# First step of each expert loop fed by products with zero-one tiles instead of gathered rows

## The chip, the core and the metric

The kernel runs on one core of one Trainium2 chip. The metric is the device time of one launch in microseconds (us), less is better; of several runs the median counts.

## What is computed

Two token groups (512 prompt tokens and 32 sample tokens, width 1024) go through two layers. Each layer is a mixer followed by a mixture of experts: a router picks, for every token, the best of four expert groups and in it two of its four experts; each of the 16 experts is a gated two-layer network of inner width 512. All of it is float32. Cut to the part that the change touches:

```python
def _moe(h, w_router, b_router, w_gate, w_up, w_down):
    ...                                   # softmax, best group, top 2 in it, weights -> combine
    for e in range(N_EXPERTS):
        act = jax.nn.silu(h @ w_gate[e]) * (h @ w_up[e])
        term = combine[..., e:e + 1] * (act @ w_down[e])
        y = term if y is None else y + term
    return y
```

The kernel does not multiply every token with every expert: it sorts the 2 x 544 picks by expert and multiplies only those rows.

## The kernel before, in words

The work of one layer's experts is 13 **steps** (PATTERN, L54). A "B" step takes up to 128 rows of one expert, a "P" step takes up to 64 rows of each of two experts. The order of the experts over the steps is found at run time from their counts, but expert 0 is always the first place and expert 1 the second (L581-582).

**Routing.** `pick(layer)` and `places(layer)` (L1589, L1640) run on VectorE (DVE) as one long chain of small operations. In its first part `places` finds each pick's row in the sorted order (`picked(0, selv)`, L1662: `posf` in float, `posi` in integers, and it raises `rows_ready`). Its second part finds the order of the experts over the steps, the rows of the outputs and a table `tabi` for the other engines; its last instruction (L1713) raises `pos_ready`.

**Gathering the rows.** On GpSimd (POOL) `dispatch(layer)` (L624) waits for `rows_ready`, then issues ten indirect DMAs that scatter the token rows of `h` into the sorted buffer `xs_d` in DRAM. When all have landed and `pos_ready` is up, `load_x(0)` and `load_x(1)` fetch the rows of steps 0 and 1 into the two halves of `xg`, which lie on the first two tiles of `h`. In layer 0 `load_ab(2)` follows: five broadcast loads (three of 512 KB, two of 128 KB) of the next norm's scale, shift and gain, needed only after the expert loop (`scale_ready(2)`, L1751). Then for each step n: `load_x(n + 2)` once TensorE has turned the rows of step n, then the store of step n's outputs to `ys_d` when ScalarE and VectorE have copied them. All of these are in one DMA queue (q0), in this order.

**Products.** On TensorE (PE) `experts(layer)` (L873) does for each step n: `pe_up(n)`; `tokens(n + 1)`, which waits for the rows and turns them with eight 128x128 transposes (`pe_tx`, L818, the rows taken at a stride of 8 columns); the first half of `pe_gate(n + 1)`; `pe_th(n)`; the second half of `pe_gate(n + 1)`; `pe_down(n)`. Ahead of the loop stand `tokens(0)` and `pe_gate(0)`. ScalarE and VectorE each copy one half of the turned rows from PSUM to `xgT` (`copy_x`); on VectorE this copy stands behind all of `places`.

In layer 0 TensorE still has products of the conditioning vectors to do (`ada`, L746) between routing and experts: `ada(6)` may start when VectorE has done `stage_ada(4)`, which stands in VectorE's program behind `places(0)`; `experts(0)` starts when VectorE has done `stage_ada(6)`.

**Weights.** SyncE (SP) feeds six slots of 2 MB in queue q1, two each for gate, up and down. For layer 0 it loads g0 and u0 when the last `ada` weights free their slots, then waits for the rows of step 1 (`xg_loaded[1]`, L451), then issues g1, d0, u1 and d1; every further load waits until the step that used its slot is through (`refill`, L457). In layer 1 all six first loads are issued before the routing. The weights are read as "(p k) f": partition p takes eight neighbouring rows, 16 KB in one piece, which is why the rows are turned at a stride of 8.

Of the kernel before, what the change touches and what calls it, by code (L numbers as in the profile page):

```python
# [12 lines left out]
def bass_yoco_stream_step(  # L13
# [7 lines left out]
    ALU, ACT, AX = mybir.AluOpType, mybir.ActivationFunctionType, mybir.AxisListType  # L21

    P = 128
# [12 lines left out]
    KC = D // P  # L36
# [73 lines left out]
    with ctx:  # L110
# [3 lines left out]
        def sem(name):  # L114
            return ctx.enter_context(nc.semaphore(name))
# [20 lines left out]
        hact = hf[:, 4608:5120]  # L136
        hactT = hT_raw[:, 0:512].rearrange("p (k t) -> p k t", k=KE)
        ysb = hT_raw[:, 512:2560].rearrange("p (b n) -> p b n", b=2)
        pair_w = hT_raw[:, 2560:3072].rearrange("p (a i j) -> p a i j", a=2, i=NE)

        rf = ring[:, :, :].rearrange("p s n -> p (s n)")
# [12 lines left out]
        S_sb = rf[:, 14336:16384].rearrange("p (b n) -> p b n", b=4)  # L154
        partT_f = rf[:, 13312:13312 + TOK]
        mf = mod[:, :, :, :].rearrange("p a s d -> p (a s d)")
        ck = [v.rearrange("p (t n) -> p t n", t=CT) for v in (mf[:, 0:2048], rf[:, 16384:18432])]
        cv = [v.rearrange("p (t n) -> p t n", t=CT) for v in (mf[:, 2048:4096], rf[:, 8192:10240])]
        bias_s = [mf[:, 4096:4096 + (CT + 1) * P], rf[:, 10240:10240 + (CT + 1) * P]]
# [125 lines left out]
        rank_done = sem("rank_done")  # L285
        rows_ready = sem("rows_ready")
        pos_ready = sem("pos_ready")
        scattered = sem("scattered")
        xg_loaded = [sem(f"xg{i}_loaded") for i in range(2)]
        y_stored = [sem(f"y{i}_stored") for i in range(2)]  # L290
# [113 lines left out]
        def _(sp):  # L404
# [21 lines left out]
            def experts(layer):  # L426
# [8 lines left out]
                def first(kind, e):  # L435

                    view, slot = views[kind][0], views[kind][1] + e
                    if layer == 0:
                        last = max(n for n in range(NADA) if ada_slot[n] == slot)
                        sp.wait_ge(unit_used, last + 1)  # L440
                    elif kind == "g":
                        sp.wait_ge(o_done, 2 * NT)
                    else:
                        sp.wait_ge(tr_done, 2 * (turned(5, TS) + 1))
                        sp.wait_ge(ab_loaded, 80 * 5)
                    load(slot, w(view, e))
# [75 lines left out]
        def _(pool):  # L522
# [99 lines left out]
            load_g(1)  # L622

            def dispatch(layer):  # L624
                pool.wait_ge(rows_ready, layer + 1)
                pool.wait_ge(tail_stored, 16)
                for t in range(NT):
# [14 lines left out]
                pool.wait_ge(scattered, 16 * 2 * NT * (layer + 1))  # L642
                pool.wait_ge(pos_ready, layer + 1)
                b = layer * NSTEP
                load_x(0)
                load_x(1)
                if layer == 0:
                    load_ab(2)

                for n in range(NSTEP):  # L650
                    if layer == 0 and n == NSTEP - 2:
                        for j in range(0, NOV, TP):
                            m = min(TP, NOV - j) * P
# [89 lines left out]
        def _(pe):  # L743
# [74 lines left out]
            def pe_tx(g, par):  # L818

                for half, done in enumerate((E.xt_act, E.xt_dve)):  # L820
# [3 lines left out]
                        last = T.transpose(pb[half][:, c * P:(c + 1) * P], xg[:, par, 4 * half + c:D:KC], ident[:, :])  # L824
                    last.then_inc(E.tx, 1)

            def tile_product(bank, lhs, rhs, start, stop):

                if len(rhs) == 1:
                    return T.matmul(bank[:, :], lhs, rhs[0], start=start, stop=stop)  # L830
                for a in range(2):
                    last = T.matmul(bank[HALF * a:HALF * a + HALF, :], lhs[:, HALF * a:HALF * a + HALF], rhs[a],  # L832
                                    start=start, stop=stop, tile_position=(0, HALF * a))
                return last

            def pe_gate(g, par, ws, ks):
                for k in ks:
                    if k == 0:
                        pe.wait_ge(E.xt_act, g + 1)
                        pe.wait_ge(E.xt_dve, g + 1)  # L840
                        if g:
                            pe.wait_ge(E.silu, g)
                    last = tile_product(pb[3], xgT[:, par, k, :], [w[:, k * DE:(k + 1) * DE] for w in ws],
                                        k == 0, k == KC - 1)
                if ks[-1] == KC - 1:
                    last.then_inc(E.gate, 1)

            def pe_up(g, par, ws):
                if g:
                    pe.wait_ge(E.hact, g)  # L850
                for k in range(KC):
                    last = tile_product(pb[4], xgT[:, par, k, :], [w[:, k * DE:(k + 1) * DE] for w in ws],
                                        k == 0, k == KC - 1)
                last.then_inc(E.up, 1)

            def pe_th(g):
                pe.wait_ge(E.hact, g + 1)
                for c in range(KE):
                    last = T.transpose(pb[2][:, c * P:(c + 1) * P], hact[:, c:DE:KE], ident[:, :])  # L859
                last.then_inc(E.th, 1)  # L860

            def pe_down(g, ws):
# [10 lines left out]
            def experts(layer):  # L873
# [7 lines left out]

                def tokens(n):
                    g = b + n
                    loads = sum(len(STEP_PLACES[i % NSTEP]) for i in range(g % 2, g + 1, 2))
# [284 lines left out]
        def _(act):  # L1169
# [84 lines left out]
            def experts(layer):  # L1254
                b = layer * NSTEP

                def copy_x(g):
                    act.wait_ge(E.tx, 2 * g + 1)
                    if g >= 2:
                        act.wait_ge(E.up, g - 1)  # L1260
                    A.activation(xgT[:, g % 2, 0:4, :], pb[0][:, :].rearrange("p (c t) -> p c t", c=4),  # L1261
                                 ACT.Copy).then_inc(E.xt_act, 1)

                copy_x(b)
                for g in range(b, b + NSTEP):
                    act.wait_ge(E.gate, g + 1)
                    if g:
                        act.wait_ge(E.hact, g)
                    A.activation(sg, pb[3][:, :], ACT.Silu).then_inc(E.silu, 1)
# [205 lines left out]
        def _(dve):  # L1475
# [164 lines left out]
            def places(layer):  # L1640
# [74 lines left out]
            def experts(layer):  # L1715
                b = layer * NSTEP

                def copy_x(g):
                    dve.wait_ge(E.tx, 2 * g + 2)
                    if g >= 2:  # L1720
                        dve.wait_ge(E.up, g - 1)
                    V.tensor_copy(xgT[:, g % 2, 4:8, :], pb[1][:, :].rearrange("p (c t) -> p c t", c=4)).then_inc(E.xt_dve, 1)  # L1722

                copy_x(b)
                for g in range(b, b + NSTEP):
                    dve.wait_ge(E.silu, g + 1)
                    dve.wait_ge(E.up, g + 1)
                    if g:
                        dve.wait_ge(E.th, g)
                    V.tensor_tensor(hact, pb[4][:, :], sg, ALU.mult).then_inc(E.hact, 1)  # L1730
                    if g + 1 < b + NSTEP:
                        copy_x(g + 1)
                    if g >= 2:
# [322 lines left out]
```

## Time and profile before

| | |
|---|---|
| median of 3 runs | 1416.54 us (1414.11 to 1419.67) |
| the profiled execution's own time | 1414.6 us |
| its span, first to last instruction | 1413.1 us, mean granted TensorE clock 0.902 |
| busy: TensorE / VectorE / ScalarE / GpSimd | 80% / 29% / 16% / 14% of the span |
| DMA traffic | 365.5 MB, mean 259 GB/s |

The span is one execution on the core; all moments below are microseconds from its start. The two expert loops are the stretches from 211 to 537 (layer 0) and from 1064 to 1378 (layer 1). A busy share over the whole span says little here: the stages have different limits, so the rows are read by stage.

### The profile page before, as it was taken

The page shows a single profiled execution, that of the slowest core. Times are in us where ns is not written, and L with a number is a line of the kernel's source. Part 1 is how long each engine was busy: PE and PEld are TensorE (multiplying, and loading weights), DVE is VectorE, ACT ScalarE, POOL GpSimd, SP SyncE. Part 2 cuts the span into 40 slices and gives each one's busy share as a digit, 9 for nine tenths or more (in the row PEclk, how much of TensorE's full clock was granted, in tenths as well). Part 3 has the DMA queues.
Part 4 walks back from the last instruction along what each step waited for, and adds up shares of the span by engine and source line. Part 5 has one row for each costly group of instructions (what it writes and reads, how often), then busy time and mean ns, then how long its engine had stood idle before and what let it go on. Part 6 is the DMA issues. An engine that isn't in the chain of part 4 may idle for free.

```text
span 1413.1 us, 12206 instructions
## 1 busy us (share of the span) xinstructions
PE 1128.2 (80%) x4592; PEld 544.1 (39%) x4592; DVE 409.1 (29%) x870; ACT 232.7 (16%) x489; POOL 191.3 (14%) x328
## 2 busy tenths in 40 slices
PE   1639856899999992999998698679727999999990
PEld 0117413344444341444554344454413444444340
DVE  1153660000101004536316555323560000000005
ACT  1002200010101002212112465211201000000001
POOL 6000021000000002000010763210020000000002
PEclk8669778999999996899999799979957999999995
DMA  9999599999899995112242401817235899998835
GB/s 314 395 385 393 224 407 362 396 424 382 348 428 344 386 341 204 52 60 65 90 178 83 121 1 40 262 39 286 104 143 182 311 424 359 372 427 336 352 125 205
DMA packets 55240, 365.52 MB, mean 259 GB/s; under 512 B 7215, under 2 KB 7711, under 8 KB 36156
## 3 DMA queue, kind: packets, MB, share of 16 engines
q1 hardware_dynamic: 32512, 285.79, 51.4%
q0 software_dynamic: 21104, 78.40, 16.1%
q8 instruction: 38, 0.62, 0.2%
q10 hardware_dynamic: 1564, 0.53, 0.1%
q14 instruction: 22, 0.18, 0.0%
HBM read 335.09 MB, written 34.33 MB: 261 GB/s over the span
## 4 chain that ended last, share of the span: by engine, by line
PE 69%; DVE 11%; DMA 10%; POOL 4%; issue 3%; ACT 2%; SPq 0%; ACTq 0%; POOLq 0%; DVEq 0%
PE pb L830 29%; PE pb L995 15%; PE pb L832 9%; DMA ring<-in_ada_w_dram 2%; DMA gainb<-in_norm_g_dram 2%; PE pb L824 2%; POOL ring L725 2%; PE pb L771 2%; DMA ring<-in_w_gate_dram 1%; DMA ada_d<-stage 1%; POOL xs_d L629 1%; DVE h L1722 1%; PE pb L1142 1%; DVE h L1531 1%; PE pb L1087 1%
## 5 line engine op out<-in xcount | busy, mean ns | idle before, releaser
L830 PE MATMUL pb<-ring,h 128*128 128x512 f32 x640 | 290.1, 603 | 19.6 <-DVE h L1722 19.6
L995 PE MATMUL pb<-ring,hT_raw 128*128 128x512 f32 x512 | 225.5, 598 | 2.7 <-DVE x L1558 1.5
L830 PEld LDWEIGHTS pb<-ring,h 128*128 128x128 f32 x640 | 119.9, 193 | 162.6 <-issue 162.6
L830 PE MATMUL pb<-ring,hT_raw 128*128 128x512 f32 x320 | 141.4, 594 | 1.5 <-issue 1.5
L995 PEld LDWEIGHTS pb<-ring,hT_raw 128*128 128x128 f32 x512 | 96.7, 192 | 118.6 <-issue 114.6
L1736 DVE COPY hT_raw<-pb 128x512 f32<-128x512 f32 x26 | 18.0, 692 | 382.1 <-PE pb L830 292.3
L757 PE MATMUL pb<-ring,cT 128*32 128x512 f32 x448 | 73.1, 795 | 69.2 <-DMA ring<-in_ada_w_dram 56.2
L832 PE MATMUL pb<-ring,h 128*64 128x512 f32 x384 | 88.1, 606 | 9.4 <-DVE h L1722 4.9
L661 POOL DMA_DIRECT2D ys_d<-hT_raw x26 | 14.1, 541 | 576.7 <-DVE hT_raw L1736 576.7
L830 PEld LDWEIGHTS pb<-ring,hT_raw 128*128 128x128 f32 x320 | 60.1, 190 | 79.4 <-issue 79.4
L1730 DVE TENSOR_TENSOR h<-pb,h 128x512 f32<-128x512 f32 x26 | 18.0, 692 | 182.8 <-PE pb L830 144.8
L1261 ACT ACTIVATE h<-pb 128x512 f32<-128x512 f32 x26 | 15.5, 597 | 312.4 <-PE pb L824 312.4
L757 PEld LDWEIGHTS pb<-ring,cT 128*32 128x32 f32 x448 | 15.8, 132 | 119.8 <-DMA ring<-in_ada_w_dram 58.4
L771 PE MATMUL pb<-ident,h 128*128 128x128 f32 (+1 forms) x160 | 28.4, 329 | 41.5 <-DVE h L1534 31.4
L824 PE MATMUL pb<-ident,h 128*128 128x128 f32 x208 | 29.7, 289 | 34.1 <-DMA h<-xs_d 34.1
L725 POOL TENSOR_TENSOR ring<-gainb,ring 128x128 f32<-128x128 f32 (+3 forms) x64 | 53.4, 861 | 19.8 <-DVE mx L1914 19.7
L832 PEld LDWEIGHTS pb<-ring,h 128*64 128x64 f32 x384 | 27.7, 138 | 60.3 <-issue 59.6
L824 PEld LDWEIGHTS pb<-ident,h 128*128 128x128 f32 x208 | 27.7, 193 | 48.7 <-DMA h<-xs_d 24.7
L771 PEld LDWEIGHTS pb<-ident,h 128*128 128x128 f32 (+1 forms) x160 | 23.7, 200 | 51.4 <-DVE h L1534 37.0
L832 PE MATMUL pb<-ring,hT_raw 128*64 128x512 f32 x192 | 42.5, 595 | 0.0
L1277 ACT ACTIVATE hT_raw<-pb 128x512 f32<-128x512 f32 x26 | 15.5, 597 | 162.6 <-PE pb L830 123.7
L1273 ACT ACTIVATE hT_raw<-pb 128x512 f32<-128x512 f32 x26 | 15.5, 597 | 147.2 <-PE pb L859 147.2
(323 smaller groups left out, 1152.5 us busy)
## 6 DMA issues: line engine op xcount, KB each, us to landing
ring<-in_w_gate_dram SPq DMA_DIRECT2D x32, 2048.0 KB, 10.6
ring<-in_w_up_dram SPq DMA_DIRECT2D x32, 2048.0 KB, 11.5
ring<-in_w_down_dram SPq DMA_DIRECT2D x32, 2048.0 KB, 12.3
ring<-in_ada_w_dram SPq DMA_DIRECT2D x24, 2048.0 KB, 10.7
ys_d<-hT_raw POOLq DMA_DIRECT2D x26, 512.0 KB, 10.5
h<-xs_d POOLq DMA_DIRECT2D x20, 512.0 KB, 15.5
ring<-in_kv_ada_w_dram SPq DMA_DIRECT2D x4, 2048.0 KB, 10.9
ring<-in_w_kvf_dram SPq DMA_DIRECT2D x4, 2048.0 KB, 16.6
```

Source lines behind the costliest of these rows:

```text
L725: g.tensor_tensor(nfm[s][b], maskp[:, SEQ - w:SEQ], nfb[:, 2 * j + s, 0:b + 1, :].rearrange("p t k -> p (t k)"), ALU.subtract).then_inc(at ...
L757: last = T.matmul(bank[32 * j:32 * j + 32, :], cT[:, 2 * u + k, :], w[:, k, j, :], start=(u == 0 and k == 0), stop=(u == 3 and k == 1), ti ...
L771: last = T.transpose(pb[2 + b][:, c * P:c * P + rows[t]], half_cols(src, t, 4 * b + c), ident[0:rows[t], 0:rows[t]])
L824: last = T.transpose(pb[half][:, c * P:(c + 1) * P], xg[:, par, 4 * half + c:D:KC], ident[:, :])
L830: return T.matmul(bank[:, :], lhs, rhs[0], start=start, stop=stop)
L832: last = T.matmul(bank[HALF * a:HALF * a + HALF, :], lhs[:, HALF * a:HALF * a + HALF], rhs[a], start=start, stop=stop, tile_position=(0, H ...
L995: last = T.matmul(bank[:, :], hT[:, k, col[t]:col[t] + P], w[:, k * 512:(k + 1) * 512], start=(k == 0), stop=(k == KC - 1))
L1261: A.activation(xgT[:, g % 2, 0:4, :], pb[0][:, :].rearrange("p (c t) -> p c t", c=4), ACT.Copy).then_inc(E.xt_act, 1)
L1273: A.activation(hactT, pb[2][:, :].rearrange("p (c t) -> p c t", c=KE), ACT.Copy).then_inc(E.hactT, 1)
L1277: A.activation(ysb[:, g % 2, 0:512], pb[5][:, :], ACT.Copy).then_inc(E.ys_act, 1)
L1730: V.tensor_tensor(hact, pb[4][:, :], sg, ALU.mult).then_inc(E.hact, 1)
L1736: V.tensor_copy(ysb[:, g % 2, 512:1024], pb[6][:, :]).then_inc(E.ys_dve, 1)
```

## The change

For step 0 of each layer the rows are no longer gathered through DRAM. VectorE builds five zero-one tiles `oneh` right behind `rows_ready`, one per tile of tokens (column n of a token's row is 1 where that token's first or second pick stands in sorted row n), by ten operations of 128x128 on an `iota` tile that POOL writes. TensorE multiplies `h` with them (`pe_pick`: 8 pieces of 128 columns times 5 token tiles, 40 products), which gives the turned rows of step 0 at once. The pieces are unbroken, so that expert 0's gate and up weights are read in another order of rows ("(k p) f", pieces of 2 KB). Since `h` is still being read, step 0 keeps its turned rows and activations in `mod`; so `load_x(0)` falls away, `load_x(1)` waits for `pe_pick`, and in layer 0 `load_ab(2)` moves from ahead of the loop to its third pass, in front of `load_x(4)`.

```diff
+        oneh = hT_raw[:, 3072:3072 + NT * P].rearrange("p (t n) -> p t n", t=NT)
+        iotap = hT_raw[:, 3072 + NT * P:3072 + NT * P + P]
+        xgT0 = mf[:, 0:1024].rearrange("p (k t) -> p k t", k=KC)
+        sg0, hact0 = mf[:, 1024:1536], mf[:, 1536:2048]
...
@@ SP, first() @@
-                    load(slot, w(view, e))
+                    if e == 0 and kind != "d":
+                        load(slot, {"g": w_gate, "u": w_up}[kind][layer, 0].rearrange("(k p) f -> p k f", p=P))
+                    else:
+                        load(slot, w(view, e))
@@ POOL, dispatch() @@
+                pool.wait_ge(logits_done, layer + 1)
+                g.iota(iotap[:, :], pattern=[[1, P]], base=0, channel_multiplier=0,
+                       allow_small_or_imprecise_dtypes=True).then_inc(iota_ready, 1)
                 pool.wait_ge(rows_ready, layer + 1)
...
                 b = layer * NSTEP
-                load_x(0)
+                pool.wait_ge(E.tx, 2 * b + 2)
                 load_x(1)
-                if layer == 0:
-                    load_ab(2)
                 for n in range(NSTEP):
+                    if layer == 0 and n == 2:
+                        pool.wait_ge(E.th, b + 1)
+                        pool.wait_ge(E.up, b + 1)
+                        load_ab(2)
...
@@ PE @@
+            def pe_pick(g):
+                pe.wait_ge(picks_ready, g // NSTEP + 1)
+                for half, done in enumerate((E.xt_act, E.xt_dve)):
+                    if g:
+                        pe.wait_ge(done, g)
+                    for c in range(4):
+                        for t in range(NT):
+                            last = T.matmul(pb[half][:, c * P:(c + 1) * P], h[0:rows[t], t, (4 * half + c) * P:(4 * half + c + 1) * P],
+                                            oneh[0:rows[t], t, :], start=(t == 0), stop=(t == NT - 1))
+                    last.then_inc(E.tx, 1)
...
-                tokens(0)
+                pe_pick(b)
                 pe_gate(b, b % 2, units(G_SLOT, 0), range(KC))
@@ DVE, places() @@
                 picked(0, selv).then_inc(rows_ready, 1)
+                dve.wait_ge(iota_ready, layer + 1)
+                for t in range(NT):
+                    last = V.tensor_scalar(oneh[:, t, :], iotap[:, :], posf[:, 0, 0, t:t + 1], None, ALU.is_equal)
+                link(last)
+                for t in range(NT):
+                    last = V.scalar_tensor_tensor(out=oneh[:, t, :], in0=iotap[:, :], scalar=posf[:, 0, 1, t:t + 1],
+                                                  in1=oneh[:, t, :], op0=ALU.is_equal, op1=ALU.add)
+                last.then_inc(picks_ready, 1)
```

The rest of the diff names the buffers of step 0 (`step_xgT`, `step_sg`, `step_hact`) where ScalarE, VectorE and TensorE use them, and counts one load less in `tokens`.

## Rows read from the trace of the kernel before

**Rows 1.** The page: its first line and the shares of the chain that ended last.
```profile
span 1413.1 us, 12206 instructions
...
PE 69%; DVE 11%; DMA 10%; POOL 4%; issue 3%; ACT 2%; SPq 0%; ACTq 0%; POOLq 0%; DVEq 0%
```
**Rows 2.** The chain in order of time (start us, us, what), both loops' entries.
```profile
211.45 10.79 DMA h<-xs_d
...
225.19 15.85 PE pb L830 x32
...
250.69 18.78 DMA ring<-in_w_gate_dram
...
323.01 17.17 PE pb L830 x40
...
1064.14 3.81 DMA h<-xs_d
...
1070.94 16.23 PE pb L830 x32
```
**Rows 3.** Timeline of VectorE (start, us, what): both entries.
```profile
202.10 1.29 DVE L1498 TENSOR_TENSOR stage<-pb,adab 128x512 f32<-128x512 f32 x2
...
212.88 0.69 DVE L1498 TENSOR_TENSOR stage<-pb,adab 128x512 f32<-128x512 f32 x1 [9.49 <-PE pb L757]
...
1047.24 0.17 DVE L1658 CAST posi<-posf 128x10 int32<-128x10 f32 x1
...
1060.73 0.18 DVE L1713 CAST tabi<-tabf 1x49 int32<-1x49 f32 x1
...
1070.00 0.69 DVE L1722 COPY h<-pb 128x512 f32<-128x512 f32 x1 [9.10 <-PE pb L824]
```
**Rows 4.** Timeline of TensorE (start, us, what, idle before): ada(6), gate(2), turns.
```profile
202.85 9.86 PE L757 MATMUL pb<-ring,cT 128*32 128x512 f32 x64 [12.97 <-DVE stage L1498]
...
269.57 5.35 PE L832 MATMUL pb<-ring,h 128*64 128x512 f32 x16 [4.45 <-DMA ring<-in_w_gate_dram]
...
316.83 1.05 PE L824 MATMUL pb<-ident,h 128*128 128x128 f32 x8
...
1067.99 1.97 PE L824 MATMUL pb<-ident,h 128*128 128x128 f32 x8 [24.46 <-DMA h<-xs_d]
```
**Rows 5.** Lines L1510 and L958: ns min/median/max, first and last start us, form.
```profile
L1510 DVE TENSOR_TENSOR bands<-bands,ident x4: 291/291/293, 33.5 to 40.2; 128x128 f32<-128x128 f32 x4
...
L958 PE MATMUL pb<-bands,h x48: 274/275/421, 106.0 to 129.1; 128*128 128x128 f32 x48
```
**Rows 6.** Timeline of the SP queue, layer 0: g0 and g1 issued.
```profile
206.55 0.34 SPq L409 DMA_DIRECT2D ring<-in_w_gate_dram  x1
...
223.39 0.33 SPq L409 DMA_DIRECT2D ring<-in_w_gate_dram  x1
```
**Rows 7.** Weight loads: 2 KB pieces (the page), 16 KB pieces (DMA from 949 to 962).
```profile
ring<-in_w_q_dram SPq DMA_DIRECT2D x2, 2048.0 KB, 9.5
...
ring<-in_w_up_dram SPq DMA_DIRECT2D x1, 2048.0 KB, 8.1
```
**Rows 8.** Timeline of POOL: the store of step 1, the load for step 4.
```profile
287.57 0.54 POOL L661 DMA_DIRECT2D ys_d<-hT_raw  x1 [27.18 <-DVE hT_raw L1736]
288.72 0.53 POOL L640 DMA_DIRECT2D h<-xs_d  x1 [0.62 <-issue]
```
**Rows 9.** DMA from 288 to 304: packets, MB, share of 16 engines; KB, us to landing.
```profile
q1 hardware_dynamic: 399, 5.78, 85.2%
q0 software_dynamic: 288, 1.05, 16.0%
...
ys_d<-hT_raw POOLq DMA_DIRECT2D x1, 512.0 KB, 10.5
h<-xs_d POOLq DMA_DIRECT2D x1, 512.0 KB, 15.5
```
**Rows 10.** DMA from 586 to 600, where `load_ab(3)` has the queues to itself.
```profile
q0 software_dynamic: 528, 1.84, 49.5%
```

More of the change, by code:

```diff
@@ L156, in bass_yoco_stream_step, with step_xgT, step_sg, step_hact @@
         mf = mod[:, :, :, :].rearrange("p a s d -> p (a s d)")
+        xgT0 = mf[:, 0:1024].rearrange("p (k t) -> p k t", k=KC)
+        sg0, hact0 = mf[:, 1024:1536], mf[:, 1536:2048]
+        def step_xgT(g):
+            return xgT[:, g % 2, :, :] if g % NSTEP else xgT0
+        def step_sg(g):
+            return sg if g % NSTEP else sg0
+        def step_hact(g):
+            return hact if g % NSTEP else hact0
         ck = [v.rearrange("p (t n) -> p t n", t=CT) for v in (mf[:, 0:2048], rf[:, 16384:18432])]
@@ L287, in bass_yoco_stream_step @@
         pos_ready = sem("pos_ready")
+        picks_ready = sem("picks_ready")
+        iota_ready = sem("iota_ready")
         scattered = sem("scattered")
@@ L842, in pe_gate @@
                             pe.wait_ge(E.silu, g)
-                    last = tile_product(pb[3], xgT[:, par, k, :], [w[:, k * DE:(k + 1) * DE] for w in ws],
+                    last = tile_product(pb[3], step_xgT(g)[:, k, :], [w[:, k * DE:(k + 1) * DE] for w in ws],
                                         k == 0, k == KC - 1)
@@ L851, in pe_up @@
                 for k in range(KC):
-                    last = tile_product(pb[4], xgT[:, par, k, :], [w[:, k * DE:(k + 1) * DE] for w in ws],
+                    last = tile_product(pb[4], step_xgT(g)[:, k, :], [w[:, k * DE:(k + 1) * DE] for w in ws],
                                         k == 0, k == KC - 1)
@@ L858, in pe_th @@
                 for c in range(KE):
-                    last = T.transpose(pb[2][:, c * P:(c + 1) * P], hact[:, c:DE:KE], ident[:, :])
+                    last = T.transpose(pb[2][:, c * P:(c + 1) * P], step_hact(g)[:, c:DE:KE], ident[:, :])
                 last.then_inc(E.th, 1)
@@ L883, in tokens @@
                     g = b + n
-                    loads = sum(len(STEP_PLACES[i % NSTEP]) for i in range(g % 2, g + 1, 2))
+                    loads = sum(len(STEP_PLACES[i % NSTEP]) for i in range(g % 2, g + 1, 2) if i % NSTEP)
                     pe.wait_ge(xg_loaded[g % 2], 16 * loads)
                     pe_tx(g, g % 2)
-                tokens(0)
+                pe_pick(b)
                 pe_gate(b, b % 2, units(G_SLOT, 0), range(KC))
@@ L1260, in copy_x @@
                         act.wait_ge(E.up, g - 1)
-                    A.activation(xgT[:, g % 2, 0:4, :], pb[0][:, :].rearrange("p (c t) -> p c t", c=4),
+                    A.activation(step_xgT(g)[:, 0:4, :], pb[0][:, :].rearrange("p (c t) -> p c t", c=4),
                                  ACT.Copy).then_inc(E.xt_act, 1)
@@ L1268, in experts @@
                         act.wait_ge(E.hact, g)
-                    A.activation(sg, pb[3][:, :], ACT.Silu).then_inc(E.silu, 1)
+                    A.activation(step_sg(g), pb[3][:, :], ACT.Silu).then_inc(E.silu, 1)
                     if g + 1 < b + NSTEP:
@@ L1721, in copy_x @@
                         dve.wait_ge(E.up, g - 1)
-                    V.tensor_copy(xgT[:, g % 2, 4:8, :], pb[1][:, :].rearrange("p (c t) -> p c t", c=4)).then_inc(E.xt_dve, 1)
+                    V.tensor_copy(step_xgT(g)[:, 4:8, :], pb[1][:, :].rearrange("p (c t) -> p c t", c=4)).then_inc(E.xt_dve, 1)
                 copy_x(b)
@@ L1729, in experts @@
                         dve.wait_ge(E.th, g)
-                    V.tensor_tensor(hact, pb[4][:, :], sg, ALU.mult).then_inc(E.hact, 1)
+                    V.tensor_tensor(step_hact(g), pb[4][:, :], step_sg(g), ALU.mult).then_inc(E.hact, 1)
                     if g + 1 < b + NSTEP:
```

## The prediction

> **What bounds the kernel now.** The chain that ended last is 69% TensorE and 10% DMA [rows 1]; a shorter way in front of TensorE pays only where TensorE really waits. So I read next the chain in order of time at the two loops' entries. In layer 0 it passes through a load of sorted rows that lands at 222.24, the first gate and up products from 225.19, and a wait for weights that lands at 269.47 [rows 2]; of that last piece TensorE sat idle for 4.45 us, before gate(2) at 269.57 [rows 4]. In layer 1 it passes through a load that lands at 1067.95 and products from 1070.94 [rows 2]; TensorE had stood idle for 24.46 us [rows 4]. So layer 1's entry is a pure wait for rows, and layer 0's entry is followed by a wait for weights, which an earlier start alone does not shorten.
>
> **Layer 1, step by step.** VectorE has the integer rows at 1047.24 + 0.17 = 1047.4 and then works on in `places` until 1060.91 [rows 3]. The ten tile operations come in between. An operation of this size alone takes 0.29 us [rows 5]: 2.9 us if each waited for the one before, which only one of them does; as the lower end I take half of that, 1.5 us, and as the value 2.0 us. `picks_ready` then comes at about 1049.5. The 40 products have the shape of L958's, 0.275 us alone [rows 5], and come as often as the turns of that shape: eight in 1.05 us, or (1.05 - 0.27)/7 = 0.11 us apart, at TensorE's upper clock level (2.4 GHz), and eight in 1.97 us, 0.22 us apart, at the lower (1.2 GHz), where the engine had been idle for 24 us before [rows 4]. So `pe_pick` takes 4.7 to 9.1 us and ends between 1054 and 1059. It hides beside `places`, which now ends at 1060.91 + 2.0 = 1062.9: VectorE's half of the copy stands behind it in program order. If `places` were shorter, up to 9.1 us would show. The copy takes 0.69 us [rows 3], and the products follow 0.25 us after it (1070.94 - 1070.69): 1063.85 instead of 1070.94, **7.1 us earlier**. Of the clock I expect nothing here: TensorE has stood idle before the copy in both kernels, so the 16.23 us of gate and up [rows 2], longer than 15.85 us in layer 0, stay. `load_x(1)` needs the scatters and `pos_ready`, as now, and starts at about 1064.2; it lands 4 to 5 us later, and step 1 wants it only at 1080. Layer 1: -6.9 us, between -9 and -5.
>
> **Layer 0, its entry.** The same 2.0 us on VectorE push `stage_ada(4)` from 202.10 to 204.1 [rows 3], and with it `ada(6)` (9.86 us [rows 4]) and `stage_ada(6)`, from 212.88 to 214.9 [rows 3]. `pe_pick` starts at 215.7 and, right behind `ada(6)`, runs at the upper level: 40 x 0.11 + 0.3 = 4.7 us, ending at 220.4; copy to 221.1, products from 221.3 instead of 225.19. Without the idle 9 us before them they should take 32 x 0.43 (17.17/40 [rows 2]) = 13.8 us instead of 15.85, so TensorE reaches the next turns 6 us earlier. Does the data keep up? g0 and u0 are issued 2.0 us later (g0 at 208.6 [rows 6]); pieces of 2 KB land after 9.5 us, of 16 KB after 8.1 us on quiet queues [rows 7]: 218, in time; I cost the pieces at nothing (1.4 us if the slack of 3 us were gone). `load_x(1)` goes out 1.15 us after `pe_pick` (the distance of two POOL issues [rows 8]), at 221.6, and lands 3.8 us later [rows 2], 1 us more beside the tail of u0: 226.4. SP waits for exactly this before it issues g1, d0, u1, d1: 3.0 us later than at 223.39 [rows 6]. That delays the weights; but `load_ab(2)` and `load_x(0)` no longer compete with them. Before, the seventh load from there (g3) landed 269.47 - 223.39 = 46.1 us later. Now I count 8.1 us for the first, six more at 2.10 MB at 427 GB/s = 4.9 us (6.83 MB in 16 us [rows 9]) and 1.3 us for a store: 38.8 us, g3 at 265.2. Gate(2) starts 4 us earlier; the bounds are 46.1 us unchanged (3 us later) and TensorE's own 6 + 4.45 - 1 = 9.4 us earlier.
>
> **Layer 0, what is moved.** `load_ab(2)` now stands in POOL's program and in q0 between the store of step 1 and `load_x(4)`. In the trace these two are issued at 287.57 and 288.72 [rows 8] and land after 10.5 and 15.5 us, at 298.1 and 304.2 [rows 9]; TensorE wants the rows of step 4 at 316.83 [rows 4]. **The slack is 12.6 us.** In this stretch q1 is full of weights: q0 gets 16.0% of the engines' time and moves 1.05 MB in 16 us, 66 GB/s with its start in it; from landing to landing 0.52 MB in 6.1 us, 85 GB/s [rows 9]. `load_ab` is 1.84 MB [rows 10]. In front of the load for step 4 it costs 1.84/85 = 21.6 to 1.84/66 = 27.8 us, thus a stall of 9.0 to 15.2 us of TensorE in `tokens(4)`; both ends move with step 1, so an earlier entry changes nothing. I take 24.6 us, between the two since the start is paid once: **a stall of 12.0 us**. q1 does not run dry meanwhile (u5, g6, d4, d5 and u6 are already issued), and behind the stall nothing is late: `load_x(5)` has a step more to go. Nothing waits for `load_ab(2)` itself before the loop's end.
>
> The Trainium skill, page "DMA: Bandwidth & Descriptors", section "Anatomy of one DMA — SWDGE (gpsimd) path", prices a GpSimd DMA at about 2 us plus its bytes at 436 GB/s. By that (an estimate from the page) the moved loads would take 4.2 us and up to 2 us more, less than the slack, and the 12.0 us of the sum would be zero. The 15.5 us for 512 KB beside a full q1 [rows 9] speak against using it here.
>
> **Sum.** -6.9 - 4.0 + 12.0 = +1.1 us on the profiled execution's own 1414.6 us: 1415.7. The median of the runs shown, 1416.54, lies 1.9 us higher; I carry that over: 1417.6 us. About 0.5%, 7.1 us, is what a measurement of this kernel can tell from no change.
>
> **The rivals.**
> *No stall.* For it: with the queues to itself `load_ab` used 49.5% of 14 us, 6.9 us of all engines [rows 10], less than the slack. It would need the engines to serve q0 ahead of q1, or q1 to have gaps; the 16.0% beside 85.2% [rows 9] speak against both. Then -6.9 - 4.0 = -10.9 us: 1405.6, faster. The page's price above leads here too. Chance 0.20.
> *A longer stall, and slower.* The broadcast loads read one row over and over, and even alone they moved only 1.84 MB in 6.9 us of engine time, 267 GB/s against 427 GB/s of the mix [rows 9, 10]; so q0 may move them more slowly than rows and stores. At 55 GB/s they take 33.4 us, the stall is 20.8 us and the sum +9.9: 1426.4. It decides from a stall of 18.0 us on (30.6 us, 60 GB/s), where the total passes 7.1 us. Against it: 66 GB/s already holds a start. Chance 0.18.
> *The forecast*, with stalls of 9 to 15 us and an entry between 3 us later and 9 us earlier, has 0.62; its bounds are -6.9 - 9.4 + 9.0 = -7.3 and -6.9 + 3.0 + 15.2 = +11.3 us, 1409 to 1428. Of it 0.54 lies within 0.5% and 0.08 above, where a stall near 15 us meets an entry that gains nothing. That the tiles don't do their work I give no chance: the first expert's rows are the sorted rows 0 to 127 by construction.
>
> **How the numbers follow.** Faster 0.20 (no stall), same 0.54, slower 0.18 + 0.08 = 0.26. The range of 1405 to 1428 reaches from the first rival's time to a little above the second's; what lies beyond (a stall of more than 22 us, an entry that gains all 9 us without a stall) is left out. The forecast's own range is 1409 to 1428.
>
> **What would show it.** In the chain of layer 1 no load of rows, VectorE's copy at about 1064 and products right after it; a `pe_pick` of 5 to 9 us that ends before `places`. In layer 0 products from 221, g1 issued at 226, gate(2) at 265. Then, at step 4, TensorE idle for about 12 us before the turns, released by the DMA into `h` from `xs_d`, with a landing of over 35 us for that load. If that idle time is missing, the forecast is wrong by its largest term; if g1 is issued later than 230, the entry of layer 0 is; if VectorE's copy in layer 1 waits for TensorE, the products were dearer than 0.22 us each.

## The result and the profile after

The changed kernel takes 1440.49 us (median of 4 runs, 1436.24 to 1445.88); the kernel before took 1418.11 us beside it (4 runs). The ratio is 1.016, 95% interval 1.0127 to 1.0192: slower by 1.6%. The prediction of 1417.6 us, with a range of 1405 to 1428, missed it.

The page's first line and chain shares stand against [rows 1]: TensorE's share of the chain grew by a point, and the span by 21.7 us.

```profile
span 1434.8 us, 12505 instructions
...
PE 70%; DVE 12%; DMA 10%; issue 3%; ACT 2%; POOL 2%; SPq 0%; ACTq 0%; DVEq 0%; POOLq 0%
```

The chain in order of time, both entries and step 4 (start us, us, what), against [rows 2]:

```profile
213.03 12.10 PE pb L860 x80
...
225.99 13.97 PE pb L867 x32
...
249.61 22.38 DMA ring<-in_w_gate_dram
...
293.33 37.27 DMA h<-xs_d
...
333.61 5.05 PE pb L867 x8
...
1069.79 21.90 PE pb L860 x80
1091.71 0.70 DVE mod L1767
1092.41 0.25 issue
1092.66 16.41 PE pb L867 x32
```

In place of the two loads of rows at the entries stands `pe_pick` (L860), 12.1 and 21.9 us of it, both on the path; and a load of rows has come in at step 4 that takes 37.27 us. TensorE's timeline (start, us, what, idle before), against [rows 4], shows what it waited for:

```profile
203.46 8.65 PE L782 MATMUL pb<-ring,cT 128*32 128x512 f32 x64 [15.34 <-DVE stage L1535]
213.03 12.08 PE L860 MATMUL pb<-hT_raw,h 128*128 128x128 f32 x80 [0.92 <-DVE stage L1535]
...
272.08 5.06 PE L869 MATMUL pb<-ring,h 128*64 128x512 f32 x16 [8.04 <-DMA ring<-in_w_gate_dram]
...
330.65 1.97 PE L849 MATMUL pb<-ident,h 128*128 128x128 f32 x8 [11.42 <-DMA h<-xs_d]
```

Look first at the count in the second line: x80, where the prediction had 40 products. VectorE's and SyncE's timelines give the two signs that the prediction had named as those that would prove it wrong (VectorE's copy waits for TensorE; g1 is issued later than 230), against [rows 3, 6]:

```profile
1091.71 0.69 DVE L1767 COPY mod<-pb 128x512 f32<-128x512 f32 x1 [8.56 <-PE pb L860]
```
```profile
232.42 0.34 SPq L426 DMA_DIRECT2D ring<-in_w_gate_dram  x1
```

The stretches of both picks, and of the products behind the stall (columns: busy time of PE, PEld, DVE, ACT, POOL, then the granted clock, DMA share and GB/s):

```profile
213.00:225.20 12.20, 12.08 (x80) 10.08 (x80) 0.04 (x1) 1.88 (x2) 0.00 (x0) 1.00 0.60 227
...
330.60:338.00 7.40, 6.37 (x15) 3.56 (x16) 0.69 (x1) 0.60 (x1) 0.00 (x0) 0.61 0.99 415
1069.80:1091.70 21.90, 21.87 (x80) 18.21 (x80) 11.87 (x44) 1.88 (x2) 7.70 (x9) 0.50 0.51 193
```

Layer 0's pick ran at TensorE's upper level (1.00, 2.4 GHz), layer 1's at the lower (0.50, 1.2 GHz) from end to end, after idle times of 10.28 and 6.33 us with two small products between them.

The timelines of TensorE cut every run into the same pieces. In the table, entry 0 goes from layer 0's routing logits (first of the ten records with 16 columns) to gate(2), loop 0 from there to the end of its last product, "between" from there to layer 1's logits (code that no run edits, though the late loads reach into its start, see e3_before_ab_late), entry 1 from those to the first gate product. All in us, from each run's profile; the last column is the time of the runs.

```
run                   entry 0   loop 0   between   entry 1   median us
before                  97.15   267.96    492.49     40.93     1418.11
changed                101.40   281.61    497.11     41.85     1440.49
e1_ab_late             101.91   268.00    498.17     41.85     1426.04
e2_before_ab_third      93.43   282.32    497.62     40.27     1430.30
e3_before_ab_late       95.54   266.28    500.29     40.20     1417.49
e4_warm                100.15   283.86    497.37     33.19     1432.71
e5_late_warm           102.09   268.67    498.37     33.20     1416.75
e6_late_warm_spfree     94.88   268.02    497.84     33.20     1412.18
e7_mixed                93.02   266.27    498.46     33.22     1409.97
e8_snake               100.64   267.66    497.37     34.07     1412.85 (one run)
e9_pick40               97.63   269.20    498.99     33.18     1412.75
e10_all                 94.77   266.29    494.03     33.18     1405.38
e11_mixed_snake         95.54   266.38    500.21     34.07     1409.30
e12_spread             101.43   268.05    497.75     41.84     1425.38
```

By these profiles the change cost 4.25 us in entry 0, 13.65 in loop 0 and 0.92 in entry 1: 18.8 us. The medians differ by 22.4, 18 to 27 by the interval, so the parts fit, but 3.6 us are not assigned to a stage. The two spans differ by 21.7 us, of which 4.6 lie in "between"; there the profile of before is 5 us shorter than most, with the same code, and its own time, 1414.6 us, lies 3.5 us below its median.

Profiles of the same code differ. Entry 0 is 100.15 to 102.09 in the five with the changed kernel's entry (changed, e1, e4, e5, e12), and 93.02 to 95.54 in four with gathered rows and no `load_ab(2)` beside them (e2, e3, e7, e11). Entry 1 of the kernel before is 40.93, but 40.27 and 40.20 in e2 and e3, because the logits took 2.11 us in the first profile and 1.23 in the others. So entry 0 can be read to about 2 us, and the gains in entry 1 named below against 40.93 are 0.7 us smaller against the other two.

### The profile page after: what moved, and what is told of

It reads as the page before. It is cut to its first block, busy times and chain, and to the rows that moved or that the text cites. A ratio compares the mean times of both kernels' runs of the same rounds, so it can differ in the third digit from the quotient of the medians.

```text
span 1434.8 us, 12505 instructions
## 1 busy us (share of the span) xinstructions
PE 1160.4 (81%) x4736; PEld 571.2 (40%) x4736; DVE 413.7 (29%) x890; ACT 232.8 (16%) x489; POOL 189.9 (13%) x328
## 3 DMA queue, kind: packets, MB, share of 16 engines
q0 software_dynamic: 20816, 77.36, 15.6%
## 4 chain that ended last, share of the span: by engine, by line
PE 70%; DVE 12%; DMA 10%; issue 3%; ACT 2%; POOL 2%; SPq 0%; ACTq 0%; DVEq 0%; POOLq 0%
PE pb L867 28%; PE pb L1032 16%; PE pb L869 8%; DMA h<-xs_d 3%; PE pb L860 2%; DMA ring<-in_ada_w_dram 2%; PE pb L796 2%; DMA ring<-in_w_gate_dram 2%; PE pb L849 2%; PE pb L1124 1%; DMA gainb<-in_norm_g_dram 1%; PE pb L1179 1%; DMA ada_d<-stage 1%; PE pb L782 1%; DVE h L1568 1%
## 5 line engine op out<-in xcount | busy, mean ns | idle before, releaser
L867 PE MATMUL pb<-ring,h 128*128 128x512 f32 x576 | 259.4, 598 | 17.9 <-DVE h L1767 17.9
L1032 PE MATMUL pb<-ring,hT_raw 128*128 128x512 f32 x512 | 226.4, 600 | 1.3 <-DVE hT_raw L1576 0.8
L867 PEld LDWEIGHTS pb<-ring,h 128*128 128x128 f32 x576 | 106.8, 191 | 144.4 <-issue 144.4
L1314 ACT ACTIVATE hT_raw<-pb 128x512 f32<-128x512 f32 x26 | 15.5, 597 | 162.6 <-PE pb L867 123.7
L1310 ACT ACTIVATE hT_raw<-pb 128x512 f32<-128x512 f32 x26 | 15.5, 597 | 152.4 <-PE pb L896 152.4
L860 PE MATMUL pb<-hT_raw,h 128*128 128x128 f32 (+1 forms) x160 | 34.0, 373 | 7.3 <-DVE hT_raw L1705 6.3
L1451 ACT ACTIVATE ring<-ring,mx 128x128 f32<-128x128 f32 (+3 forms) x64 | 35.4, 554 | 24.7 <-DVE mx L1959 24.7
## 6 DMA issues: line engine op xcount, KB each, us to landing
h<-xs_d POOLq DMA_DIRECT2D x18, 512.0 KB, 15.6
```

The source lines that it names most:

```text
L860: last = T.matmul(pb[half][:, c * P:(c + 1) * P], h[0:rows[t], t, (4 * half + c) * P:(4 * half + c + 1) * P], oneh[0:rows[t], t, :], start ...
L1032: last = T.matmul(bank[:, :], hT[:, k, col[t]:col[t] + P], w[:, k * 512:(k + 1) * 512], start=(k == 0), stop=(k == KC - 1))
L1310: A.activation(hactT, pb[2][:, :].rearrange("p (c t) -> p c t", c=KE), ACT.Copy).then_inc(E.hactT, 1)
L1451: A.activation(S_sb[:, i, 0:w], S_sb[:, i, 0:w], ACT.Exp, bias=mx[:, i, 0:1], scale=-1.0, accum_out=rs[:, j % 2, TP * s + b, 0:1]).then_in ...
```

## The experiments

**The stall alone.** First theory: the loss is `load_x(4)` queueing behind the moved `load_ab(2)`. Rival: the dearer products and later weights of the entry.

```diff
-                    if layer == 0 and n == 2:
+                    if layer == 0 and n == NSTEP - 2:
                         pool.wait_ge(E.th, b + 1)
                         pool.wait_ge(E.up, b + 1)
                         load_ab(2)
```

> The changed kernel with one edit: the five broadcast loads of load_ab(2) stand in the second-to-last pass of layer 0's loop, behind the last load of rows. Stall theory (TensorE's wait in tokens(4) is the queueing of load_x(4) behind these loads): the idle time of 11.4 us before the turns of step 4 falls to under 1.5 us, the landing of load_x(4) comes back from 37 us to 13 to 18 us, layer 0's loop ends 12 to 15 us earlier, time 1425 to 1429 us. Rival, pick theory (most of the loss comes from the dearer products and the later weights in layer 0, and TensorE would wait at the next weights instead): the loop ends at most 5 us earlier, 1435 to 1440 us. Under the stall theory a loss of 7 to 11 us against the kernel before stays, for the entries to explain.

1426.04 us (6 runs), ratio to before 1.0068 (1.0047 to 1.0089). The timeline of TensorE, gate(2) and the turns of step 4:

```profile
275.68 5.39 PE L869 MATMUL pb<-ring,h 128*64 128x512 f32 x16 [8.00 <-DMA ring<-in_w_gate_dram]
...
322.98 1.05 PE L849 MATMUL pb<-ident,h 128*128 128x128 f32 x8
```

And the landing of the load for step 4, from the DMA view of 292 to 311 (KB, us to landing):

```profile
h<-xs_d POOLq DMA_DIRECT2D x1, 512.0 KB, 15.6
```

The wait before the turns is gone, the load lands after 15.6 us, loop 0 is 13.6 us shorter: the stall theory holds for 14.4 us of the 22.4. The wait of 8 us at gate(2) has stayed, and of the 7.8 us that are left to before the entries hold 5.7 (4.8 and 0.9 by the table); 2.8 more stand right behind loop 0 (see e3_before_ab_late).

**The same load in the kernel before,** at the third pass (the diff) and, in a run of its own, at the second-to-last (`n == NSTEP - 2`):

```diff
                 load_x(1)
-                if layer == 0:
-                    load_ab(2)
...
+                    if layer == 0 and n == 2:
+                        load_ab(2)
```

> The kernel before with one edit: load_ab(2) moved to the third pass, in front of load_x(4), as the change has it; no products with zero-one tiles. Stall theory: an idle time of 10 to 13 us before the turns of step 4, the load behind it landing after 34 to 39 us; at the entry gate(2) loses its wait of 4.45 us, since 1.84 MB no longer compete with g1 to g3; sum +6 to +10 us, 1424 to 1428 us. Rival (the stall needs the changed entry, where weights start 9 us later and so stay ahead longer): the stall is under 5 us and the time is 1413 to 1419 us.

1430.30 us, ratio 1.0099 (1.007 to 1.0128): slower than expected, by the right mechanism.

```profile
264.56 3.66 PE L832 MATMUL pb<-ring,h 128*64 128x512 f32 x16 [0.98 <-DVE h L1722]
...
323.28 1.97 PE L824 MATMUL pb<-ident,h 128*128 128x128 f32 x8 [12.99 <-DMA h<-xs_d]
```

The stall, 12.99 us, needs nothing of the changed entry; the rival falls. Entry 0 is 3.7 us shorter, since gate(2) finds its weights. The expectation left out that the products behind the stall run slowly at first (5.59 us for eight records where 3.67 is usual).

> The kernel before with load_ab(2) moved behind the last load of rows in layer 0 (second-to-last pass). Stall theory with the relief that the prediction's sum used: gate(2) starts up to 4.45 us earlier and nothing waits later, 1412 to 1415 us. Rival (weights at the entry are bound by what TensorE gives free, not by the competing loads): gate(2) within 1 us of 269.6 and 1416 to 1419 us.

1417.49 us (10 runs), ratio 0.999 (0.9975 to 1.0006): no difference that can be measured, where 1412 to 1415 was expected and the rival had 1416 to 1419. In its profile gate(2) no longer waits for weights and entry 0 is 1.6 us shorter, but gate(2) starts at 268.72, within the rival's 1 us, since TensorE came to it later. And what loop 0 and its entry gain is lost right behind the loop. TensorE's first turns there, and POOL's first gathering of outputs, which waits for the last store (each in the kernel before, then here):

```profile
560.97 1.97 PE L771 MATMUL pb<-ident,h 128*128 128x128 f32 x8 [23.44 <-DVE h L1534]
...
560.99 1.97 PE L771 MATMUL pb<-ident,h 128*128 128x128 f32 x8 [25.99 <-DVE h L1534]
```
```profile
542.78 1.01 POOL L678 DMA_INDIRECT ring<-ys_d,posi  x1 [3.34 <-DMA ys_d<-hT_raw]
...
542.65 1.00 POOL L678 DMA_INDIRECT ring<-ys_d,posi  x1 [5.73 <-issue]
```

The last product ends 2.5 us earlier, but the last store lands after 5.3 us instead of 2.9, and the turns behind the loop start at the same moment as before. The late loads stand ahead of that store in q0, and the copies issued right behind them land after 27.2 us instead of 20.3 (median of two). So they are not free there: this idle time is 24.8 to 26.5 us in eight of the nine kernels with the late loads (23.7 in e6_late_warm_spfree), and 23.4 to 24.0 in the five others, e12_spread among them.

**Layer 1: the granted clock.** TensorE is kept busy ahead of pick by turns of the identity tile that nobody reads:

```diff
+            def warm(m):
+                for _ in range(m):
+                    T.transpose(pb[2][:, 0:P], ident[:, :], ident[:, :])
...
             route(1)
+            warm(44)
             ranks(1)
+            warm(30)
             experts(1)
```

> The changed kernel with 44 extra 128x128 turns of the identity tile into an unused bank between routing and ranks of layer 1, and 30 more between ranks and the products with zero-one tiles; nothing else differs, layer 0 keeps its stall. Clock theory (pick took 21.9 us in layer 1 and 12.1 us in layer 0 because TensorE had stood idle and its granted clock was 0.50): pick in layer 1 takes 11.5 to 14 us, ends before places or within 1 us of it, gate(14's first step) starts 7 to 9 us earlier and gate and up take 14 us instead of 16.4: 1429 to 1434 us. Rival (the products are slow there for another reason, such as the tiles' place in memory or VectorE's work beside them): pick stays over 20 us and the time is 1438 to 1442 us, more by whatever the turns delay ranks.

(The "14's first step" there is gate(13), layer 1's first.) 1432.71 us, 7.8 us less than the changed kernel, ratio to before 1.0106 (1.0079 to 1.0134).

```profile
1056.14 5.02 PE L912 MATMUL pb<-ident 128*128 128x128 f32 x44
...
1067.42 5.20 PE L912 MATMUL pb<-ident 128*128 128x128 f32 x30
1073.96 12.08 PE L860 MATMUL pb<-hT_raw,h 128*128 128x128 f32 x80 [1.33 <-DVE hT_raw L1711]
1088.16 15.63 PE L867 MATMUL pb<-ring,mod 128*128 128x512 f32 x32 [2.12 <-DVE mod L1773]
```

Stretches of the 30 turns' first half and of pick's, columns as above:

```profile
1067.40:1070.00 2.60, 2.60 (x15) 2.60 (x15) 1.92 (x11) 0.00 (x0) 0.00 (x0) 0.50 0.01 3
...
1074.00:1080.00 6.00, 6.00 (x41) 5.03 (x41) 5.28 (x21) 0.00 (x0) 4.48 (x6) 1.00 0.91 359
```

Pick now has a granted clock of 1.00 and takes 12.08 us, as in layer 0; it ends beside `places`, and TensorE then waits for VectorE: entry 1 is 33.19 us, 8.7 less than in the changed kernel and 7.7 less than before. Gate and up gained less than expected, 15.63 us against 16.41. The clock theory holds.

> The changed kernel with both edits of the runs before it: load_ab(2) behind the last load of rows, and the extra turns of the identity tile that keep TensorE busy ahead of pick in layer 1. If stall and clock are separate causes, the gains add: 1426.0 - 7.8 = 1418.3 us, between 1415 and 1421 us, no difference from the kernel before; layer 1's entry (logits to first products) about 33 us against 40.9 before, layer 0's entry still 3 us longer and gate(2) still waiting about 8 us for weights. Rival (the two overlap, or the gain in layer 1 is given back in its loop): over 1422 us.

Both edits together: 1416.75 us (10 runs), ratio 0.9975 (0.9955 to 0.9994). Stall and clock add up. Entry 0 is still 102 us, and gate(2) waits 6.94 us.

**Layer 0: who holds the weights back.** One line more than the run before it:

```diff
-                    if layer == 0 and n == 2:
-                        sp.wait_ge(xg_loaded[1], 16)
                     first(kind, int(e))
```

> As the run before it, and SyncE no longer waits for the rows of step 1 before it issues g1, d0, u1 and d1 of layer 0. Theory of the late weights (what is left in layer 0 is that these rows now wait for pick, so that the weights start 9 us later and gate(2) waits 8 us): gate(2) loses its wait, 5 to 8 us less than the run before it, 1410 to 1414 us; the load of step 1's rows, now beside full weight queues, lands after 9 to 12 us instead of 4, about when TensorE wants it. Rival (the weights take the engines from the rows, as at the stall of step 4): TensorE waits for the rows of step 1 or 2 by as much, and the time stays at 1416 to 1420 us.

1412.18 us (10 runs), ratio 0.9951 (0.9928 to 0.9975), 4.6 us below the run before it (5 to 8 were expected). TensorE's gate(2), and from the DMA view of 229 to 246 the load for step 1 (KB, us to landing):

```profile
268.24 3.65 PE L867 MATMUL pb<-ring,h 128*64 128x512 f32 x16 [0.98 <-DVE h L1771]
```
```profile
h<-xs_d POOLq DMA_DIRECT2D x1, 512.0 KB, 11.5
```

The wait for weights is gone and entry 0 is 7.2 us shorter than in e5_late_warm, 5.3 us shorter than in the quickest of the five profiles with the changed entry. The load now shares the engines with the weights and takes 11.5 us where it took 5.7 in the changed kernel, just in time. In the changed kernel, then, pick delayed the rows of step 1, SyncE waited for those rows, and gate(2) paid for it.

**Products in layer 1 alone.** Layer 0 gets back `load_x(0)`, `tokens(0)` and its weights' order; the turns of the identity tile and the late `load_ab(2)` stay.

```diff
...
-                pe_pick(b)
+                if layer == 0:
+                    tokens(0)
+                else:
+                    pe_pick(b)
...
```

> Products with zero-one tiles in layer 1 alone, with the extra turns ahead of them; layer 0 enters its loop as the kernel before does (gathered rows, weights in the order of the others), with load_ab(2) behind the last load of rows. Theory (the products gain only where TensorE waits for nothing but rows, layer 1; in layer 0 they cost an entry 3 us longer and later weights): layer 1's entry 33 us against 40.9, layer 0's entry as before with gate(2) not waiting, sum -8 to -11 us, 1407 to 1411 us. Rival (layer 0's products are no loss once the stall is gone): no faster than the run with both layers, 1416 us or more.

1409.97 us (5 runs), ratio 0.9929 (0.9901 to 0.9956): faster than before by 0.7%, and 7.5 us below e3_before_ab_late, which enters layer 0 in the same way.

```profile
268.12 3.65 PE L871 MATMUL pb<-ring,h 128*64 128x512 f32 x16 [1.87 <-DMA ring<-in_w_gate_dram]
```

Gate(2) waits 1.87 us for weights, against an expectation of none.

**The order of the tiles.** Every second chunk takes the five token tiles backwards, so that the products of the 32-row tile come four records at a time and TensorE changes its number of rows about half as often:

```diff
-                        for t in range(NT):
+                        for i, t in enumerate(range(NT) if c % 2 == 0 else range(NT - 1, -1, -1)):
...
```

> The changed kernel with load_ab(2) late, and every second chunk of pick taking the five token tiles in reverse order, so that the 32-row tile's products of two chunks stand side by side and TensorE changes its number of rows 8 times instead of 15. If the change of row count is what costs (chunks take 1.50 us where ten products at 0.112 us would take 1.12): pick 10.3 to 10.8 us in layer 0 and 19 to 20 us in layer 1. If the 32-row products themselves cost more: 12.1 and 21.9 us as in the changed kernel. One look; the time should stay within 3 us of 1426.

Timelines of both picks, and stretches of layer 1's:

```profile
216.24 10.74 PE L860 MATMUL pb<-hT_raw,h 128*128 128x128 f32 x80 [0.92 <-DVE stage L1535]
...
1056.80 14.10 PE L860 MATMUL pb<-hT_raw,h 128*128 128x128 f32 x80 [6.34 <-DVE hT_raw L1705]
```
```profile
1060.80:1062.80 2.00, 2.00 (x11) 2.00 (x11) 1.73 (x9) 0.00 (x0) 1.39 (x3) 0.50 0.95 379
1062.80:1064.80 2.00, 2.00 (x11) 1.66 (x11) 1.76 (x8) 0.00 (x0) 1.53 (x2) 0.67 1.00 389
1064.80:1066.80 2.00, 2.00 (x18) 1.88 (x18) 1.76 (x8) 1.08 (x2) 1.55 (x2) 1.00 0.97 377
```

Layer 0 as expected: 1.3 us less with the same 80 records, so the change of row count is what costs. Layer 1 not: 14.10 us, 5 us below the nearer theory, because the granted clock rose from 0.50 to 1.00 within pick. The time, 1412.85 us in a single run, is 13 us below the 1426 expected; entry 1, 7.8 us shorter than in e1_ab_late, holds most of that, and one run doesn't settle the rest.

> Products with zero-one tiles in layer 1 alone, tiles of every second chunk in reverse order, without the extra turns of the identity tile; load_ab(2) late. The one look showed the granted clock rise from 0.50 to 1.00 inside pick with this order (14.1 us) where it stayed at 0.50 for 21.9 us with the other. If the order does that: pick 13.5 to 15 us, layer 1's entry 34 us, 1409 to 1412 us. Rival (that look was chance): pick 19 to 20 us, entry 39 to 40 us, 1414 to 1418 us.

1409.30 us (6 runs), ratio 0.994 (0.9921 to 0.9958), entry 1 34.07, and pick takes 14.10 us again:

```profile
1054.32 14.10 PE L862 MATMUL pb<-hT_raw,h 128*128 128x128 f32 x80 [6.33 <-DVE hT_raw L1711]
```

The rival falls: with this order the clock came up in both kernels, with the other (changed kernel, e1_ab_late, e12_spread) it stayed at the lower level for 21.9 us. What in the order does it was not tried.

**The count that the prediction used.** Late `load_ab(2)`, and only as many products as leave 40 records; the rows from the other token tiles are left out of step 0:

```diff
-                        for t in range(NT):
+                        ts = ((0, 2, 4), (0, 2))[half]
+                        for t in ts:
...
```

> The changed kernel with load_ab(2) late and pick cut to 20 products, which the trace records as 40 (three of the five token tiles for the first four chunks, two for the others); the rows of expert 0 from the tiles left out are thus missing from step 0. This is the number that the prediction counted. Theory of the count (the prediction's steps hold, only the products were twice as many): pick takes 4.7 to 6 us in layer 0 and 9 to 10.5 us in layer 1 at the lower clock, ends there before places, and the first products start 7 to 9 us earlier than with all products (logits to products 33 to 34 us in layer 1); in layer 0 gate(2) waits under 3 us for weights; time 1409 to 1413 us, faster than the kernel before. Rival (the entries lose for another reason, as the later one-hot tiles or the weights in pieces of 2 KB): over 1418 us.

1412.75 us (10 runs), ratio 0.9965 (0.9947 to 0.9983), inside the expected time, but not all of it by the expected way:

```profile
216.74 6.27 PE L861 MATMUL pb<-hT_raw,h 128*128 128x128 f32 x40 [0.92 <-DVE stage L1536]
...
270.21 6.62 PE L870 MATMUL pb<-ring,h 128*64 128x512 f32 x16 [8.29 <-DMA ring<-in_w_gate_dram]
...
1057.37 11.08 PE L861 MATMUL pb<-hT_raw,h 128*128 128x128 f32 x40 [6.33 <-DVE hT_raw L1706]
```

In layer 1, 40 records at the lower clock hide beside `places`: entry 1 is 33.18 us, 7.75 below before. In layer 0 the wait at gate(2) was to fall below 3 us and is 8.29: with half the products entry 0, 97.63 us, is still no shorter than before's 97.15. The start of products moved; the weights' start did not move enough (g1 is issued at 229.94, before at 223.39 [rows 6]).

**The five loads one by one,** in the third to seventh pass, each ahead of that pass's load of rows (a `load_ab_part(2, n - 2)` in place of `load_ab(2)`):

> The changed kernel with the five loads of load_ab(2) spread over the third to seventh pass of layer 0's loop, one ahead of each pass's load of rows; everything else as in the changed kernel. Queue theory (a load of 512 KB costs the rows behind it 5 to 7 us, less than the slack of about 12 us, and only the five together exceed it): no wait ahead of the turns of steps 4 to 8, load_x(4) lands after 20 to 24 us, 1424 to 1429 us, as with all of them late. Rival (any broadcast load ahead of a load of rows stalls TensorE): 1430 us or more with several short waits.

1425.38 us (6 runs), ratio 1.0054 (1.0034 to 1.0074). From the DMA view of 291 to 316:

```profile
mod<-ada_d POOLq DMA_DIRECT2D x1, 512.0 KB, 16.8
h<-xs_d POOLq DMA_DIRECT2D x1, 512.0 KB, 21.9
```

The turns of step 4 in TensorE's timeline:

```profile
320.80 1.05 PE L867 MATMUL pb<-ident,h 128*128 128x128 f32 x8
```

The load behind one part lands after 21.9 us instead of 15.6, 6.3 us for 512 KB, and TensorE waits neither here nor before the turns of steps 5 to 8. It is the sum of the five, not their kind, that passes the slack.

**All mends together.**

> All four mends on the changed kernel: load_ab(2) late, extra turns ahead of pick in layer 1, SyncE not waiting for the rows of step 1, and the tiles of every second chunk in reverse order. If the causes are separate: the run without the last of them took 1412.2 us and layer 0's pick is 1.3 us shorter, layer 1's is hidden anyway: 1410 to 1412 us. Rival (an earlier gate(1) meets rows or weights that are not there): 1412 us or more, with a wait ahead of the turns of step 1 or of gate(1).

1405.38 us (7 runs, 1403.28 to 1411.45), ratio 0.9928 (0.9904 to 0.9952), faster than expected. In its profile the entries are those of e6_late_warm_spfree to 0.1 us; pick of layer 0 is 1.3 us shorter, but the logits took 0.85 us longer. "Between" is 3.8 us shorter, which is not of the edit's making, so what makes it faster than expected isn't shown. It and e7_mixed beat both kernels; their ratios don't tell them apart.

## Why the prediction was wrong

*The number of products: the step that failed.* "The 40 products" of `pe_pick` are 80 records, since a product of float32 leaves two MATMUL records and a turn leaves one. The rows of before held this: gate and up of one step are 16 products in the code and x32 in [rows 2], and the prediction's own price per product of gate and up, 17.17/40, was one per record. The turns' pace of 0.11 to 0.22 us was right per record; taken per product it halved `pe_pick`: 12.08 us measured instead of 4.7 in layer 0, 21.89 instead of at most 9.1 in layer 1. Twice the count makes 9.0 us (80 at 0.112) and 17.0 (80 at 0.213); the other 3 and 5 us are the changes of row count between the token tiles (last section), a cost that the prediction didn't have.

*Layer 1, -6.9 us predicted, +0.9 measured.* (The prediction's own steps give 7.1 us; the 0.2 between is not explained there.) The mechanism was right and the size wrong: with 40 records (e9_pick40) entry 1 gains 7.75 us, with the upper clock (e4_warm) 7.7. Twice the products at the lower clock don't fit beside `places`, and VectorE's copy waited 8.56 us for them. The prediction's "up to 9.1 us would show" had priced the lower clock, but only once.

*Layer 0's entry, -4.0 us predicted, +4.25 measured.* Here the count isn't all. Pick took 7.4 us longer. With half the products (e9_pick40) the entry still gains nothing, because the small terms all fell on the dear side: pick starts at 216.7 instead of 215.7 and takes 6.27 us instead of 4.7, `load_x(1)` follows 1.6 us later and needs 5.3, and SyncE issues g1 at 229.94 where 226.4 was forecast. The stream behind it was priced well: 38.8 us to g3's landing forecast, 39.6 in the changed kernel (232.42 to 271.99). The prediction had seen that SyncE waits for these rows and put 3.0 us on it; measured it is 9.0 (232.42 against 223.39 [rows 6]), 10.8 counted from the logits, and e6_late_warm_spfree shows that this wait alone was worth 5 to 7 us of entry 0. The pieces of 2 KB made nothing wait: g0 landed after 8.8 us (8.3 before), u0 after 10.7 (11.0), and gate and up took 13.97 us, 13.8 forecast. What the pieces cost by themselves isn't shown, since before 2.07 MB of q0 ran beside those two loads and now 0.12.

*The moved loads, a stall of 12.0 us predicted, 11.42 measured.* This step held: the landing took 37.27 us (over 35 was the sign), 21.8 more than the 15.5 of [rows 9], the low end of the forecast's 21.6 to 27.8. The load itself was also issued 2.4 us later behind its store (3.5 us instead of 1.15 [rows 8]), since POOL issues five loads in between; that wasn't priced. That the two together come so near the 24.6 us of the forecast is luck. Not priced either: after the idle time the turns and the next eight records take 1.97 and 5.05 us instead of 1.05 and 3.67, 2.3 us more, at a mean granted clock of 0.61. With both, loop 0 lost 13.65.

The Trainium skill, page "DMA: Bandwidth & Descriptors", section "Anatomy of one DMA — SWDGE (gpsimd) path", has a GpSimd DMA take about 2 us plus its bytes at 436 GB/s; by that (an estimate from the page) these loads make no stall. Beside a full queue of weights the trace doesn't agree: 37.27 us for 512 KB with 1.84 MB ahead of it. The prediction's rival "no stall" fell; "a longer stall" fell too, as the loads moved at 1.84 MB in 21.8 us, 84 GB/s, and not at 55.

*The sum.* -6.9 - 4.0 + 12.0 = +1.1 became +0.9 + 4.25 + 13.65 = +18.8 us. Of the error of 17.7 us the entries hold 16.1, and the stall's slow restart the rest. The range failed because it treated the stall as the open question and pick's duration, on which both gains rested, as known within a factor that it named but didn't carry over: no rival had a pick that doesn't hide. Of the 0.26 for slower, 0.18 stood on a longer stall, which didn't come; the other 0.08 had an entry of layer 0 that gains nothing, and came nearest.

## What to carry to other kernels

Count instructions in the trace's own unit: find a line whose products in the code you can count, divide its records by them, and price new work per record. Where an edit fills an idle stretch, price it at the clock that TensorE is granted after that stretch, and look at what stands behind the new work's end in other queues (here SyncE's weights behind POOL's rows). A load that nobody needs for 200 us belongs where its queue has slack: five loads together cost 14 us; the same five spread out made TensorE wait for no rows, and late they held up the last store (by 2.4 us in e3_before_ab_late).

## What the runs showed of the hardware beyond that

Where the row count of the products changes (128 to 32 or back), the first record behind the change and the one after it come 0.20 to 0.21 us behind the record before them instead of 0.112 (upper clock; 0.35 to 0.38 instead of 0.213 at the lower). So a chunk of ten records with one 32-row tile takes 1.50 us, not 1.12, and a change costs 0.19 us: e8_snake, with 8 changes instead of 15, took 10.74 us instead of 12.08. The Trainium skill, page "TensorEngine Tiling (Array Packing)", section "Key Properties", says that a change of tiling mode drains TensorE. The trace agrees in that every change between the forms that it records as 128*128 and 32*128 costs time; a drain as such it doesn't show.

Layer 1's pick was busy for 21.87 of 21.90 us and its granted clock stayed at 0.50, while the same 80 records in another order brought it to 1.00 after some 7 us, in two kernels. In e4_warm the 44 turns, behind 0.8 us without work and the logits' ten small records, ran at 1.00 from the start; the 30 behind `ranks`, after 5.33 us without work, began at 0.50, and the clock rose before pick. What separates these cases was not tried further.
